# The states of a state-space mixer stored by planes of the step index, its powers moved behind the stacking of u, and a third piece of the gated projection between the halves

## The chip, the cores and the metric

One Trainium2 chip, one of its cores. The time is device microseconds from launch to end; the time before is the median of three executions.

## The reference

A trunk of two layers over 256 tokens of width 1024. The first layer mixes tokens with a diagonal complex state-space model and a gated projection, the second with differential attention; behind each stands a mixture of 32 experts in 4 groups. Only the first mixer is touched:

```
u = rms_norm(x) @ w_in                         # 64 groups of 16 channels
lam_bar = exp(lam * dt)                        # per group, 64 complex states
b_bar = ((lam_bar - 1) / lam) * b
s[t] = lam_bar * s[t-1] + b_bar @ u[t]         # complex
y = real(c @ s) + d_skip * u
val, gate = split(gelu(y) @ w_glu, 2)
x = x + val * sigmoid(gate)
```

## The kernel before

All is fp32 in the mixer. Four engines and SyncE (SP, which only issues transfers) run programs of their own and meet at semaphores; each program's order is written out by hand, and an engine that waits holds up everything behind. `then_inc` raises a semaphore, `wait_ge` waits for a value.

The 256 time steps are taken four at a time (SB = 4), so that the recurrence runs over M = 64 steps, m = 8 h + l: h counts eight segments, l eight steps within one (SEG = 8). Two groups make a pair, 32 pairs, worked on in four octets o of eight (OCT). One pair's two times 64 states fill the 128 partitions; re and im are i = 0, 1. A half is two octets.

- `inputs(c)`, TensorE: u for 128 channels into PSUM. `stack`: copies u out of PSUM into U4, 4 steps x 32 channels on the partitions, 64 copies, 56 of them on ScalarE (ACT) and the last 8 on VectorE (DVE).
- `weights(o)`, VectorE, makes input weights W1 from powers of lam_bar; `turn_w1`, TensorE, turns them; `keep_w1T`, ScalarE, copies them back. GpSimd (POOL) makes the output weights W2 for all octets at the same time, and clears tiles before and after.
- mu: lam_bar^4 to its eighth powers, VectorE: three calls of `powers`, each six products (`cmul`).
- `drive(o)`, TensorE: the inputs of the recurrence into PSUM (v_done, two per octet); `keep_x(o)`, ScalarE, copies them to X.
- `taps(o)`, TensorE: the direct part of y within four steps; `skips(half)`, VectorE, adds d_skip; `own(half)`, ScalarE, copies the result to Fw.
- `local_states(half)`, VectorE: within each segment x[l+1] += mu x[l], seven steps of five operations (`advance`: three products, two sums). `carries(half)`: from segment to segment, six steps of the same form on 32 elements. `carried(o)`: adds to each state what its segment was handed, four products and two sums per octet, and raises `state`.
- `y(o)`, TensorE: U4 times Fw, which needs `f_ready`, then X times W2, which needs `state`. Then `gelu` (ScalarE), `turn_g` (TensorE), `keep_g` (ScalarE).
- `glu(n, ks)`, TensorE: the gated projection for token tile n % 2 and column half n // 2, k in ks of eight. y(0) and y(1) give k 0 to 3, y(2) and y(3) give k 4 to 7. Behind it sigmoid (ScalarE) and product and sum (VectorE, `mixed`).

X lies as [re/im, pair, m]: neighbouring l are adjacent, and the operands of local_states (one l, all h) step by 8 words.

Behind the mixer come norm, router and experts. 2 MB units of expert weights go through nine slots; the first eight units wait for tiles of the mixer that they overwrite, the next for experts that are done.

## Time and profile before

| | us |
|---|---|
| median of 3 (lowest, highest) | 950.24 (949.27, 950.56) |
| profiled execution: time, span | 950.29, 948.5 |
| TensorE busy | 736.2 |
| VectorE busy | 302.0 |
| ScalarE busy | 186.5 |
| GpSimd busy | 75.1 |
| mixer: end of its last projection | 207.7 |

The busy times are sums over the whole span, and the stages have different limits; what counts is which wait ends last in a stage. The chain is the way back from the last instruction, at each step to what released it. The clock is TensorE's granted clock as a share of 2.4 GHz. Durations of pipelined operations overlap, so steps are read from one start to the next.

### The profile page before, as it was taken

Reading aid. Unit: us, or ns where it says so; the run is one execution under the profiler, and the core shown is the slowest. Engines: PE = TensorE matmul, PEld = TensorE weight load, DVE = VectorE, ACT = ScalarE, POOL = GpSimd, SP = SyncE. Lnnn points to the kernel's source line nnn. Section 1 sums busy time; section 2 is a strip of 40 time slices with the busy share of each in tenths; the row PEclk is TensorE's granted clock in tenths of the full one; section 3 lists DMA queues with packets and bytes.
Section 4 is the critical chain, followed back from the end, with each engine's and each line's share of the span. In section 5 each row is a group of like instructions: output and inputs, shape, how many; then the busy total and the mean of one; then the engine's idle time right before and its main releaser. Section 6 shows DMA issues by size and latency. Waiting matters only on the chain.

```text
span 948.5 us, 15405 instructions
## 1 busy us (share of the span) xinstructions
PE 736.2 (78%) x6273; PEld 432.3 (46%) x6273; DVE 302.0 (32%) x702; ACT 186.5 (20%) x398; POOL 75.1 (8%) x64
## 2 busy tenths in 40 slices
PE   2969485994697668676699996666398999996696
PEld 1859354432554334343344444333354555553453
DVE  5792997115421001100421533223711111211112
ACT  3653430123110000000300324113210111110012
POOL 6691000002100000000000000001200000000000
PEclk9986797995699888878899997877599999999899
DMA  9520502934399999999990472016089990499991
GB/s 262 148 96 1 179 1 75 419 130 197 103 425 425 424 424 423 424 424 423 390 338 1 178 266 89 0 41 247 1 352 423 420 402 0 158 422 424 422 418 63
DMA packets 58074, 238.40 MB, mean 251 GB/s; under 512 B 17624, under 2 KB 17824, under 8 KB 33440
## 3 DMA queue, kind: packets, MB, share of 16 engines
q1 hardware_dynamic: 56560, 235.25, 62.2%
q0 software_dynamic: 576, 2.10, 0.6%
q8 instruction: 41, 0.67, 0.3%
q10 hardware_dynamic: 880, 0.23, 0.1%
q14 instruction: 17, 0.14, 0.0%
HBM read 236.53 MB, written 1.05 MB: 250 GB/s over the span
## 4 chain that ended last, share of the span: by engine, by line
PE 49%; DVE 19%; SPq 16%; DMA 10%; ACT 3%; issue 2%; ACTq 0%; DVEq 0%
SPq L369 16%; PE ps L1573 9%; PE ps L1504 9%; DMA work<-in_moe_w_down 6%; PE ps L1539 5%; PE ps L1439 4%; PE ps L1486 4%; PE ps L1546 4%; DMA ring<-in_moe_w_down 3%; PE ps L1638 3%; PE ps L1360 1%; PE ps L1295 1%; PE ps L1468 1%; DVE work L961 1%; DVE work L962 1%
## 5 line engine op out<-in xcount | busy, mean ns | idle before, releaser
L1504 PE MATMUL ps<-ring,work 128*32 128x256 f32 x1824 | 148.5, 421 | 34.9 <-DMA ring<-in_moe_w_up 24.0
L1504 PEld LDWEIGHTS ps<-ring,work 128*32 128x32 f32 x1824 | 79.9, 121 | 79.9 <-issue 54.9
L1154 DVE TENSOR_TENSOR work<-ps,work 128x256 f32<-128x256 f32 x21 | 12.9, 616 | 300.4 <-PE ps L1504 300.4
L1504 PE MATMUL ps<-work 128*32 128x256 f32 x864 | 87.1, 425 | 27.5 <-DMA ring<-in_moe_w_up 10.8
L1546 PE MATMUL ps<-work 128*128 128x512 f32 x168 | 77.7, 605 | 0.0
L1486 PE MATMUL ps<-work,hT 128*128 128x128 bf16 x736 | 71.2, 227 | 6.7 <-DVE work L1104 6.7
L1504 PEld LDWEIGHTS ps<-work 128*32 128x32 f32 x864 | 45.5, 122 | 62.7 <-issue 44.3
L1573 PE MATMUL ps<-ring,hT 128*128 128x512 f32 x160 | 70.4, 593 | 0.0
L1539 PE MATMUL ps<-ring,work 128*32 128x512 f32 x496 | 65.5, 595 | 6.1 <-DMA work<-in_moe_w_down 4.4
L1486 PE MATMUL ps<-work 128*128 128x128 bf16 x368 | 68.3, 227 | 0.0
L1486 PEld LDWEIGHTS ps<-work,hT 128*128 128x128 bf16 x736 | 59.6, 102 | 15.8 <-issue 8.6
L1439 PE MATMUL ps<-ring,xr 128*128 128x512 f32 x128 | 55.3, 593 | 0.5 <-issue 0.5
L1546 PEld LDWEIGHTS ps<-work 128*128 128x128 f32 x168 | 30.2, 189 | 47.7 <-issue 30.1
L706 ACT COPY work<-ps 128x512 f32<-128x512 f32 x21 | 12.3, 585 | 169.6 <-PE ps L1515 169.6
L1573 PEld LDWEIGHTS ps<-ring,hT 128*128 128x128 f32 x160 | 29.7, 190 | 34.1 <-issue 34.0
L1439 PEld LDWEIGHTS ps<-ring,xr 128*128 128x128 f32 x128 | 24.2, 190 | 30.4 <-issue 30.4
L703 ACT ACTIVATE work<-ps 128x256 f32<-128x256 f32 x21 | 8.1, 383 | 150.3 <-PE ps L1504 150.3
L1486 PEld LDWEIGHTS ps<-work 128*128 128x128 bf16 x368 | 37.6, 102 | 0.0
L1161 DVE COPY work<-ps 128x512 f32<-128x512 f32 x21 | 14.5, 692 | 71.6 <-PE ps L1539 71.6
L1295 PE MATMUL ps<-con,xr 128*128 128x128 f32 x64 | 14.6, 404 | 27.7 <-DVE xr L864 16.7
L1539 PEld LDWEIGHTS ps<-ring,work 128*32 128x32 f32 x496 | 16.7, 109 | 40.5 <-issue 39.4
L451 POOL DMA_DIRECT2D gains<-in_final_norm_g x1 | 0.5, 530 | 400.4 <-DVE x L1255 400.4
(288 smaller groups left out, 990.0 us busy)
## 6 DMA issues: line engine op xcount, KB each, us to landing
ring<-in_moe_w_gate SPq DMA_DIRECT2D x24, 2048.0 KB, 25.3
ring<-in_moe_w_down SPq DMA_DIRECT2D x23, 2048.0 KB, 15.4
ring<-in_moe_w_up SPq DMA_DIRECT2D x17, 2048.0 KB, 23.1
work<-in_moe_w_up SPq DMA_DIRECT2D x15, 2048.0 KB, 22.9
work<-in_moe_w_down SPq DMA_DIRECT2D x9, 2048.0 KB, 27.6
work<-in_moe_w_gate SPq DMA_DIRECT2D x8, 2048.0 KB, 25.9
ring<-in_attn_w_qkv SPq DMA_DIRECT2D x5, 2048.0 KB, 21.2
ring<-in_ssm_w_glu SPq DMA_DIRECT2D x4, 2048.0 KB, 8.8
```

The source lines that it names most:

```text
L369: sp.dma_start(places[slot_of(i)].rearrange("p (e n) -> p e n", e=2), src).then_inc(here, 16)
L706: act.copy(turned_both, ps[:, 7, :]).then_inc(back_ready, 1)
L1154: TTo(hid.rearrange("s (k p) -> s p k", k=2), ps[:, 7, 0:256].rearrange("s (p k) -> s p k", k=2), sil.rearrange("s (p k) -> s p k", k=2), ...
L1161: dve.tensor_copy(yy[:, 0:512], ps[:, 6, :]).then_inc(y0_ready, 1)
L1295: ins = pe.transpose(ps[:, (4 if i else 0) + k // 2, 256 * (k % 2) + P * tt:256 * (k % 2) + P * tt + P], xr[:, tt, k, :], ident)
L1439: ins = mm(ps[:, 4 + 2 * (n % 2) + half, :], gT[:, k, tt * P:(tt + 1) * P], win[u][:, k, :], start=(k == 0), stop=(k == KD - 1))
L1486: ins = mm(ps[:, 4 + k // 4, P * (k % 4):P * (k % 4) + P], parts[i][:, tt, k, :], sel[:, tt, :], start=(tt == 0 and i == 0), stop=(tt == T ...
L1504: ins = mm(ps[s, 6 + j // 2, 0:256], xg[:, k, s], pairs[slots[e // 2]][:, e % 2, k, :], start=(k == 0), stop=(k == KD - 1))
L1539: ins = mm(ps[s, 6 + half, :], hidT[:, P * k + 32 * e:P * k + 32 * e + 32], downs[slots[e // 2]][:, e % 2, k, 512 * half:512 * half + 512] ...
L1546: ins = mm(ps[:, 2 * tt + half, :], swT[:, P * tt:P * tt + P], yy[:, 512 * half:512 * half + 512], start=False, stop=True, skip_group_chec ...
L1573: ins = mm(ps[:, c if tt == 0 else c % 2, :], hT[:, k, tt * P:(tt + 1) * P], win[slot][:, k, :], start=(k == 0), stop=(k == KD - 1))
L1638: ins = mm(ps[:, bank, :], oT[:, k, b * P:(b + 1) * P], win[slot][:, k, :], start=(k == 0), stop=(k == KD - 1))
```

## The change

- **Planes.** X becomes [re/im, l, pair, h], so that one l of all h and pairs is contiguous. U4 takes its columns in the order (l, h); `stack` and `keep_g` do the reordering. carried() writes its result to a tile of its own, Xs, as [re/im, pair, (l h)], which y() reads. Xs lies in slots 4 and 5 of the ring, so the first expert units wait for y_done.
- **Order on VectorE.** weights(2), weights(3) and the eight stack copies come ahead of the powers mu. VectorE copies the inputs of octets 0 and 1 to X itself (`inputs_kept`), ScalarE those of octets 2 and 3. skips(0) goes between the fourth and fifth local step, skips(1) ahead of the carries.
- **Order on TensorE.** drive(2) ahead of the last turn, taps(0) and taps(1) ahead of drive(3). Taps now lie in banks 6 and 7.
- **Projection.** glu(2, k 0 to 3) goes ahead of y(2); the tiles are finished in the order 0, 2, 1, 3.
- **Start.** Half of W2 is cleared by VectorE at the very start, the other half by POOL behind the norm; ssm_d gets a semaphore of its own.

```diff
-        X = part(12288, 64 * M).rearrange("p (i r m) -> p i r m", i=2, r=PAIRS)
+        X = part(12288, 64 * M).rearrange("p (i l r h) -> p i l r h", i=2, l=SEG, r=PAIRS)
...
+        Xs = [pre[:, 6144 + 1024 * n:7168 + 1024 * n].rearrange("p (i r m) -> p i r m", i=2, r=OCT) for n in range(PAIRS // OCT)]
...
+        GLU_OUT = (4, 6, 0, 4)
+        GLU_ORDER = (0, 2, 1, 3)
...
-            ups = ps[:, b, :].rearrange("p (c m s) -> p c m s", c=2, s=SB)
-            dst = U4[32 * j:32 * j + 32, :, :].rearrange("p (c a) m -> p c a m", a=4)[:, 2 * b:2 * b + 2, quad, :]
-            return copy(dst, ups[32 * quad:32 * quad + 32, :, :, SB - 1 - j])
+            ups = ps[:, b, :].rearrange("p (c h l s) -> p c l h s", c=2, l=SEG, s=SB)
+            dst = U4[32 * j:32 * j + 32, :, :].rearrange("p (c a) (l h) -> p c a l h", a=4, l=SEG)[:, 2 * b:2 * b + 2, quad, :, :]
+            return copy(dst, ups[32 * quad:32 * quad + 32, :, :, :, SB - 1 - j])
...
+        def inputs_kept(copy, o, b):
+
+            src = ps[:, 2 * (o % 2) + b, :].rearrange("p (r i l h) -> p i l r h", r=4, i=2, l=SEG)
+            pr = slice(OCT * o + 4 * b, OCT * o + 4 * b + 4)
+            for i in range(2):
+                copy(X[:, i, 0, pr, 1:SEG], src[:, i, SEG - 1, :, 0:SEG - 1])
+                ins = copy(X[:, i, 1:SEG, pr, :], src[:, i, 0:SEG - 1, :, :])
+            return ins
...
-            sp.wait_ge(state, 4)
+            sp.wait_ge(y_done, 4)
...
-            sp.wait_ge(glu_done, 2)
+            sp.wait_ge(glu_done, 3)
...
-            clear(part(4096, 8192), 8)
+            pool.wait_ge(normed, 2)
+            clear(part(8192, 4096), 4)
...
+            pool.wait_ge(half_clear, 1)
...
-            dma(drep[0:8, :], a["ssm_d"][0].rearrange("(c p) -> c p", p=P), s_lam)
+            dma(drep[0:8, :], a["ssm_d"][0].rearrange("(c p) -> c p", p=P), s_d)
...
-            act.wait_ge(s_lam, 64)
+            act.wait_ge(s_lam, 48)
...
             keep_w1T(2, 0)
-            keep_x(0)
             keep_w1T(2, 1)
             keep_w1T(3, 0)
-            keep_x(1)
             keep_w1T(3, 1)
             keep_x(2)
...
-                act.copy(gT[:, 2 * o:2 * o + 2, :].rearrange("p c (m s) -> p c s m", s=SB),
-                         ps[:, o, :].rearrange("p (s c m) -> p c s m", s=SB, c=2)).then_inc(g_ready, 1)
+                for c in range(2):
+                    ins = act.copy(gT[:, 2 * o + c, :].rearrange("p (h l s) -> p s l h", h=SEG, s=SB),
+                                   ps[:, o, :].rearrange("p (s c l h) -> p c s l h", s=SB, c=2, l=SEG)[:, c])
+                ins.then_inc(g_ready, 1)
...
+            for k in range(4):
+                ins = dve.memset(part(4096 + 1024 * k, 1024), 0.0)
+            ins.then_inc(half_clear, 1)
...
+            weights(2)
+            weights(3)
+            dve.wait_ge(u_done, 8)
+            for n in range(8):
+                stack(dve.tensor_copy, 3, n).then_inc(u4_ready, 1)
             link(dve.tensor_copy(mu[:, 0:2, 0, :], Pw[:, 0:2, 4, :]))
             powers(mu, 1, 1, 0, 0)
             powers(mu, 2, 2, 1, 0)
             powers(mu, 4, 4, 3, 0)
             link(TS(mu[:, 2, :, :], mu[:, 1, :, :], -1.0, None, ALU.mult))
-            weights(2)
-            weights(3)
-            dve.wait_ge(u_done, 8)
-            for n in range(8):
-                stack(dve.tensor_copy, 3, n).then_inc(u4_ready, 1)
+            for o in range(2):
+                for b in range(2):
+                    dve.wait_ge(v_done, 2 * o + b + 1)
+                    link(inputs_kept(dve.tensor_copy, o, b))
+                    dve.sem_inc(v_kept_x, 1)
...
+            def skips(half):
+
+                dve.wait_ge(k_done, 2 * half + 2)
+                taps = ps[:, 6 + half, :].rearrange("p (q n) -> p q n", q=KD // 2)[:, :, 0:PC]
+                TTo(taps, taps, skip[:, 4 * half:4 * half + 4, :], ALU.add).then_inc(k_ready, 1)
+
...
-                seg = X[:, :, rs, :].rearrange("p i r (h l) -> p i r h l", l=SEG)
                 tmp = [v[:, 0:256].rearrange("p (i r h) -> p i r h", i=2, r=16) for v in (scanP, scanQ)]
-                dve.wait_ge(v_kept_x, 4 * half + 4)
+                if half:
+                    dve.wait_ge(v_kept_late, 4)
                 for l in range(1, SEG):
                     n = SEG if l < SEG - 1 else SEG - 1
-                    dst = seg[:, :, :, :, l + 1] if l < SEG - 1 else seg[:, :, :, 1:SEG, 0]
+                    dst = X[:, :, l + 1, rs, :] if l < SEG - 1 else X[:, :, 0, rs, 1:SEG]
                     by = lambda i: spread(spread(mu[:, i, 0, rs], 1, 2), 3, n)
-                    advance(dst, seg[:, :, :, 0:n, l], tmp[0][:, :, :, 0:n], tmp[1][:, :, :, 0:n], by)
+                    advance(dst, X[:, :, l, rs, 0:n], tmp[0][:, :, :, 0:n], tmp[1][:, :, :, 0:n], by)
+                    if l == 4 and half == 0:
+                        skips(0)
...
-                seg = X[:, :, pr, :].rearrange("p i r (h l) -> p i r h l", l=SEG)
                 flat = hT[:].rearrange("p k t -> p (k t)")
                 n = 2 * OCT * SEG * (SEG - 1)
-                tmp = [flat[:, n * k:n * k + n].rearrange("p (i r h l) -> p i r h l", i=2, r=OCT, h=SEG) for k in range(2)]
-                by = lambda i: spread(mu[:, i, 0:SEG - 1, pr].rearrange("p n r -> p r n"), 2, SEG)
-                start = lambda i: spread(seg[:, i, :, :, 0], 3, SEG - 1)
+                tmp = [flat[:, n * k:n * k + n].rearrange("p (i l r h) -> p i l r h", i=2, l=SEG - 1, r=OCT) for k in range(2)]
+                by = lambda i: spread(mu[:, i, 0:SEG - 1, pr], 3, SEG)
+                start = lambda i: spread(X[:, i, 0, pr, :], 1, SEG - 1)
                 for i in range(2):
                     TTo(tmp[0][:, i], start(i), by(0), ALU.mult)
                     ins = TTo(tmp[1][:, i], start(1 - i), by(1 if i else 2), ALU.mult)
                 link(ins)
-                dst = X[:, :, pr, :].rearrange("p i r (h l) -> p i (r h) l", l=SEG)[:, :, :, 1:SEG]
-                for v in tmp:
-                    link(TTo(dst, dst, v.rearrange("p i r h l -> p i (r h) l"), ALU.add))
+                dst = X[:, :, 1:SEG, pr, :].rearrange("p i l r h -> p i l (r h)")
+                if o == 0:
+                    dve.wait_ge(w2_ready, 4)
+                for i in range(2):
+                    dve.tensor_copy(Xs[o][:, i, :, 0:SEG], X[:, i, 0, pr, :])
+                link(TTo(dst, dst, tmp[0].rearrange("p i l r h -> p i l (r h)"), ALU.add))
+                for i in range(2):
+                    ins = TTo(Xs[o][:, i, :, SEG:64].rearrange("p r (l h) -> p l r h", h=SEG), X[:, i, 1:SEG, pr, :], tmp[1][:, i], ALU.add)
+                link(ins)
                 dve.sem_inc(state, 1)
...
                 local_states(half)
                 if half == 0:
-                    skips(0)
+                    skips(1)
                 carries(half)
-                if half == 0:
-                    skips(1)
                 carried(2 * half)
...
-                done = {(0, 1): 2, (1, 0): 4, (1, 1): 6, (2, 0): 8, (3, 0): 10, (3, 1): 12}
+                done = {(0, 1): 2, (1, 0): 4, (1, 1): 6, (2, 0): 8, (3, 0): 10, (3, 1): 14}
...
+            drive(2)
             turn_w1(3, 1)
-            drive(2)
+            taps(0)
+            taps(1)
             drive(3)
-            for o in range(4):
-                taps(o)
+            taps(2)
+            taps(3)
...
-                        ins = mm(rows(r), X[:, i, OCT * o + r, :], W2[:, i, OCT * o + r, :], start=False, stop=(i == 1),
+                        ins = mm(rows(r), Xs[o][:, i, r, :], W2[:, i, OCT * o + r, :], start=False, stop=(i == 1),
...
+            glu(0, range(4))
             pe.wait_ge(f_ready, 32)
-            glu(0, range(4))
             glu(1, range(4))
+            glu(2, range(4))
             y(2)
             y(3)
             turn_g(2)
             turn_g(3)
             glu(0, range(4, KD))
...
+            glu(2, range(4, KD))
             glu(1, range(4, KD))
             pe.wait_ge(mixed, 1)
-            glu(2, range(KD))
-            pe.wait_ge(mixed, 2)
             glu(3, range(KD))
 
```

VectorE behind weights(1), with what each row waits for (dve_steps is its own chain): before, the powers (ring<-ring; the first and the last shown) come first, then weights(2) and (3), the stack copies, and the first local step.

```order
L945 COPY ring<-work 128x2x32 [waits dve_steps]
L893 TENSOR_TENSOR ring<-ring 128x32 [waits dve_steps]
...
L949 TENSOR_SCALAR ring<-ring 128x256 [waits dve_steps]
L931 TENSOR_TENSOR ring<-ps,ring 128x384 [waits w1_turned,dve_steps]
...
L935 TENSOR_TENSOR ring<-ring,ps 64x8x3x16
L335 COPY gains<-ps 32x2x64 [waits dve_steps,u_done]
L335 COPY gains<-ps 32x2x64 x7
L958 TENSOR_TENSOR hT<-work,ring 128x256 [waits v_kept_x]
```

Now the last product of weights(3), the stack copies, the powers, the input copies, the first local step.

```order
L953 TENSOR_TENSOR ring<-ring,ps 64x8x3x16
L340 COPY gains<-ps 32x2x64 [waits dve_steps,u_done]
L340 COPY gains<-ps 32x2x64 x7
L968 COPY ring<-work 128x2x32
L911 TENSOR_TENSOR ring<-ring 128x32 [waits dve_steps]
...
L972 TENSOR_SCALAR ring<-ring 128x256 [waits dve_steps]
L347 COPY work<-ps 128x4x7 [waits v_done,dve_steps]
L348 COPY work<-ps 128x7x32
L347 COPY work<-ps 128x4x7
...
L348 COPY work<-ps 128x7x32
L981 TENSOR_TENSOR hT<-work,ring 128x256 [waits dve_steps]
```

The powers' 19 rows moved from ahead of two weights() to behind the stack copies, and 16 input copies stand between them and the recurrence.

TensorE from the seventh input projection (L1316) on, before: turns (L1348), drives (L1360), turns, drives, then the first taps (L1377).

```order
L1348 MATMUL ps<-con,ring 128x128 x8
L1316 MATMUL ps<-hT,ring 128x256 x8
L1348 MATMUL ps<-con,ring 128x128 x16
L1360 MATMUL ps<-gains,ring 128x64 x32
L1348 MATMUL ps<-con,ring 128x128 x16
L1360 MATMUL ps<-gains,ring 128x64 x32
L1377 MATMUL ps<-ring,work 32x32
L1377 MATMUL ps<-ring,xr 32x32
L1377 MATMUL ps<-work 32x96
L1377 MATMUL ps<-work,xr 32x96
```

Now (lines are 29 higher):

```order
L1377 MATMUL ps<-con,ring 128x128 x8
L1344 MATMUL ps<-hT,ring 128x256 x8
L1377 MATMUL ps<-con,ring 128x128 x16
L1389 MATMUL ps<-gains,ring 128x64 x32
L1377 MATMUL ps<-con,ring 128x128 x8
L1389 MATMUL ps<-gains,ring 128x64 x16
L1377 MATMUL ps<-con,ring 128x128 x8
L1406 MATMUL ps<-ring,work 32x32
L1406 MATMUL ps<-ring,xr 32x32
L1406 MATMUL ps<-work 32x96
```

drive(2) comes ahead of the last turn, and taps follow it at once; the fourth drive stands behind 64 rows of taps.

TensorE from y(1)'s state part (L1418) on, before: gelu's turns (L1426), two pieces of the projection (L1439), y(2), y(3), turns, the rest.

```order
L1418 MATMUL ps<-work 64x128 x16
L1426 MATMUL ps<-con,work 128x128 x8
L1439 MATMUL ps<-ring,xr 128x512 x16
L1412 MATMUL ps<-work,gains 64x128 x8
L1418 MATMUL ps<-work 64x128 x16
L1412 MATMUL ps<-work,gains 64x128 x8
L1418 MATMUL ps<-work 64x128 x16
L1426 MATMUL ps<-con,work 128x128 x8
L1439 MATMUL ps<-ring,xr 128x512 x48
```

Now:

```order
L1449 MATMUL ps<-work,ring 64x128 x16
L1457 MATMUL ps<-con,work 128x128 x8
L1470 MATMUL ps<-ring,xr 128x512 x24
L1443 MATMUL ps<-work,gains 64x128 x8
L1449 MATMUL ps<-work,ring 64x128 x16
L1443 MATMUL ps<-work,gains 64x128 x8
L1449 MATMUL ps<-work,ring 64x128 x16
L1457 MATMUL ps<-con,work 128x128 x8
L1470 MATMUL ps<-ring,xr 128x512 x40
```

Eight products moved from behind y(2) and y(3) to ahead of them: 24 + 40, where there were 16 + 48.

## Rows read from the trace of the kernel before

**Rows 1.** The page: the span, and the chain's shares by engine.

```profile
span 948.5 us, 15405 instructions
...
PE 49%; DVE 19%; SPq 16%; DMA 10%; ACT 3%; issue 2%; ACTq 0%; DVEq 0%
```

**Rows 2.** The chain in order of time: start us, us, what.

```profile
163.66 0.60 PE ps L1426 x4
...
166.48 41.22 PE ps L1439 x96
...
252.04 7.11 PE ps L1504 x128
...
283.91 8.10 SPq L369
```

**Rows 3.** Timeline, VectorE, 85 to 125: start us, us, line, operation, idle before.

```profile
89.91 0.62 DVE L958 TENSOR_TENSOR hT<-work,ring 128x256 f32<-128x256 f32 x1 [17.82 <-ACT work L607]
...
107.81 0.20 DVE L958 TENSOR_TENSOR hT<-work,ring 128x32 f32<-128x32 f32 x1
...
113.24 0.30 DVE L1006 TENSOR_TENSOR ps<-ps,work 128x128 f32<-128x128 f32 x1
```

**Rows 4.** Timeline, TensorE, 125 to 145: y and the first half of the projection.

```profile
125.20 3.33 PE L1418 MATMUL ps<-work 128*64 128x128 f32 x32 [1.63 <-DVEq L1000]
...
130.36 13.97 PE L1439 MATMUL ps<-ring,xr 128*128 128x512 f32 x32 [0.50 <-issue]
...
144.26 1.58 PE L1412 MATMUL ps<-work,gains 128*64 128x128 f32 x16
```

**Rows 5.** Timeline, 0 to 25: the start of the program on POOL and VectorE.

```profile
6.95 7.51 POOL L463 MEMSET work<- 128x1024 f32 x8
...
8.90 0.93 DVE L842 TENSOR_SCALAR work<-work 32x128 f32<-32x128 f32 x1
...
14.46 4.08 DVE L864 SCALAR_TENSOR_TENSOR xr<-x,small,gains 128x1024 f32<-128x1024 f32 x2
...
20.02 0.21 DVE L870 TENSOR_SCALAR work<-work 32x128 f32<-32x128 f32 x1
```

**Rows 6.** Timeline, TensorE, and line 1377: projection, turns, drives, taps.

```profile
55.18 1.04 PE L1348 MATMUL ps<-con,ring 128*128 128x128 f32 x8
...
56.05 3.62 PE L1316 MATMUL ps<-hT,ring 128*128 128x256 f32 x16
...
88.50 7.26 PE L1360 MATMUL ps<-gains,ring 128*128 128x64 f32 x64
...
L1377 PE MATMUL ps<-work,xr x64: 246/246/246, 96.0 to 104.7; 128*32 128x96 f32 x64
```

**Rows 7.** Timeline, VectorE, 45 to 72: powers, weights(2), stacking.

```profile
45.61 0.74 DVE L945 COPY ring<-work 128x64 f32<-128x64 f32 x1
...
53.89 1.25 DVE L893 TENSOR_TENSOR ring<-ring 128x128 f32<-128x128 f32 x1
...
60.43 0.56 DVE L931 TENSOR_TENSOR ring<-ps,ring 128x384 f32<-128x384 f32 x1
...
69.60 2.48 DVE L335 COPY gains<-ps 32x128 f32<-32x128 f32 x8 [0.15 <-DVE ring L935]
```

**Rows 8.** Timeline, POOL, 71 to 76: clearing behind its products.

```profile
71.67 3.62 POOL L463 MEMSET work<- 128x1024 f32 x4 [0.15 <-POOL work L489]
```

**Rows 9.** Timeline, VectorE, 148 to 154: carrying into one octet.

```profile
148.36 0.92 DVE L994 TENSOR_TENSOR hT<-work,ring 128x448 f32<-128x448 f32 x1
...
151.79 2.22 DVE L999 TENSOR_TENSOR work<-work,hT 128x896 f32<-128x896 f32 x2
```

**Rows 10.** Windows: us from:to, length, busy of each engine, TensorE's clock, DMA, GB/s.

```profile
79.00:86.00 7.00, 7.00 (x35) 7.00 (x35) 0.00 (x0) 3.02 (x6) 0.00 (x0) 0.50 0.00 0
...
105.00:110.00 5.00, 0.00 (x0) 0.00 (x0) 0.30 (x1) 1.92 (x7) 0.81 0.75 274
```

**Rows 11.** Line 335, stacking: count, ns min/median/max, first to last start, forms.

```profile
L335 ACT COPY gains<-ps x56: 253/257/259, 39.7 to 61.7; 32x128 f32<-32x128 f32 x56
```

More of the change, by code:

```diff
@@ L673, in _ @@
             keep_g(3)
[L675 to L679 removed]
+            for turn_no, n in enumerate(GLU_ORDER):
+                act.wait_ge(glu_done, turn_no + 1)
+                if turn_no >= 1:
+                    act.wait_ge(mixed, turn_no)
+                act.activation(sig[:, 0, :], ps[:, GLU_OUT[n] + 1, :], ACT.Sigmoid).then_inc(sig_ready, 1)
             def moe(l):
@@ L711, in moe @@
                 return passes_through(act, l)
-            norm(1, mixed, 3, 4)
+            norm(1, mixed, 2, 4)
             total = moe(0)
@@ L1322, in turn_params @@
                 pe.wait_ge(lam_ready, 1)
+                pe.wait_ge(s_d, 16)
                 for n in range(4):
@@ L1432, in glu @@
                 for k in ks:
-                    if n < 2 and k % 2 == 0:
+                    if k % 2 == 0:
                         pe.wait_ge(g_ready, k // 2 + 1)
```

44 lines of the change are left out of this document (18 added, 26 removed).

## The prediction

> **What bounds the kernel now.** I read the page first: the span is 948.5 us and its chain is half TensorE, a fifth VectorE, the rest weight streaming [rows 1]. Then the chain in order of time: up to the router it goes through the state-space mixer, which ends with the gated projection at 166.48 + 41.22 = 207.7 us; the stream of expert weights enters only at 283.9, after the first passes have freed their slots [rows 2]. Nothing in the mixer waits for the stream, and the stream's start hangs on the mixer's end. So what the mixer saves is saved at the end, one for one, and I price the mixer alone.
>
> Inside it, VectorE's timeline is the thing to see. The recurrence starts at 89.91, after 17.82 us of idleness; its seven local steps last until 107.6, 2.55 us each; the carries take 5.4 (107.81 to 113.24) [rows 3]. Carrying into one octet takes (151.79 - 148.36) + 2.22 + 0.2 = 5.85 [rows 9], twice in a half. That makes 17.7 + 5.4 + 11.7 = 35 us a half, in one unbroken run of short operations, each waiting for the one before. TensorE waits for the second half too: the U part of y(2) is done at 145.84 [rows 4] and the chain has y(3) end only at 163.66 [rows 2].
>
> **The start of the program.** POOL clears 8 pieces from 6.95 to 14.46 [rows 5]. Meanwhile a scalar operation on VectorE over 32x128 takes 0.93 (0.21 where POOL is idle), and five such stand ahead of the norm's products, which start at 14.46 [rows 5]. At most 5 x 0.72 = 3.6 us are to be had; some hides behind ScalarE's squares. The change puts four of the pieces on VectorE at the very start, ahead of its first work, and four on POOL behind the norm. I take 2.2 us for everything up to the stacking, ends 0 and 2.9. ssm_d on a semaphore of its own is in that figure.
>
> The Trainium skill (SBUF — State Buffer, "SBUF: two separate sides") says that VectorE's two-port operations and GpSimd share a port pair as a lock held for a whole instruction. The trace agrees (0.93 against 0.21 us). [...]
>
> **Up to the recurrence.** The last input projection now ends at 56.05 + 3.62 - 2.2 = 57.5 [rows 6]. weights(2) and weights(3) come ahead of the powers. weights(3) waits for the fourth turn, which ended at 56.2, so 54.0 [rows 6]; one takes (69.60 - 60.43)/2 = 4.6 [rows 7], so 58.6. The eight stack copies take 2.5 [rows 7]: 61.1, where before they ended at 72.1. The powers follow. While POOL multiplies, copy and first two powers took 45.61 to 53.89, 8.3 us [rows 7]; POOL's products end at 71.67 - 2.2 = 69.5 [rows 8], so this stretch stays dear and ends at 69.4. The third power is six products of 128; a free one has 0.30 [rows 3], overlapped 0.2, so 1.4. One scalar operation beside POOL's clearing takes 1.0 (as the 0.93). The powers end at 71.8. Moving them saves no work. It lets drive(0) start at 61 and not 72.
>
> Then VectorE copies the inputs of octets 0 and 1 itself: 16 copies, 4 each of four times. No row has 28 or 224 elements. With 0.15 + 1.04 ns per element (0.30 for 128 [rows 3], 0.56 for 384 [rows 7], 1.1 for 896 [rows 9]), a set is 2 x 0.18 + 2 x 0.38, less what overlaps, 0.88; four are 3.5 (2.5 to 6 if the PSUM reads are stepped at half rate). TensorE's drives are done long before: 64 passes take 7.26 at the full clock [rows 6], so 61.1 to 68.4. The recurrence starts at **75.3**, 14.6 earlier.
>
> **The recurrence.** In the old layout neighbours in h lie 32 bytes apart: 256 elements take 0.62, 448 take 0.92, about 1.8 ns each, where contiguous ones have 1.04 [rows 3, 9]. By planes the three products and sums of 256 take 0.42 and the two of 128 lose 0.09 each: 0.8 less per step, 1.75. Seven steps are 12.1 (was 17.7). The carries keep their stride and step: 5.4. Carrying into an octet: four products 0.92 to 0.62, minus 1.2; added are two copies of 64 (0.25), and the second sum is now two instructions (0.05): 5.85 to 4.95.
>
> The Trainium skill (Vector Engine (DVE) Microarchitecture Reference, "Measured stream behaviour on trn2") gives about 1.04 ns per column for adjacent words and up to 2.5 where a stream steps by a few words. By that a step would save 1.3 and not 0.8; only the first half's seven steps lie on the path, so the sum would be 921.4. The rows have 1.8, and they decide.
>
> **New waits.** skips(0) stands after the fourth step, at 75.3 + 7.0 = 82.3, and waits for taps 0 and 1. drive(2) can start when octet 0 is copied, 73.6; +3.6, a turn 1.0, two taps of 2.3 (four of them keep TensorE from 95.7 to 104.9, and of their last kind of matmul the first starts at 96.0, the last at 104.7 [rows 6]): 82.9. With the sum itself 83.3; three more steps, 88.4. skips(1) now stands ahead of the carries and waits for all taps: drive(3) 86.5, two taps 91.1. That is a new stall of 2.7 us on VectorE, with the carries, states and y(0) queued behind it. Carries 91.5 to 96.9; states 1 and 2 at 101.9 and **106.8** (before 125.1, just ahead of the matmuls at 125.20 [rows 4]). ScalarE copies octets 2 and 3 and then both blocks of taps, free at about 102, in time.
>
> **The gated projection.** From state 2 to its first matmul are 5.25 us (125.1 to 130.36 [rows 4]). TensorE's clock adds: after the taps it is idle and falls, as in 105 to 110 (0.81, on its way to 0.5) [rows 10]. y(0)'s X part then runs at 1.2 GHz, 5.3 and not 3.33, and y(1)'s U part falls behind state 2: +2.3 (0 to 3). Start 114.4; with gelu and turning as before. Three pieces of k 0 to 3 are 24 products at 13.97/16 = 0.87 [rows 4]: 20.9, till 135.3. State 4 is there at 106.8 + 12.1 + 5.4 + 9.9 = 134.2, so in the second half VectorE no longer bounds. y(2) and y(3), each 1.58 + 3.33 [rows 4]: 145.1. Turning took 163.66 to 166.48 [rows 2]: 147.9. Left are 40 products at 41.22/48 = 0.86 [rows 2], 34.4: **182.3** against 207.7. The third piece alone shortens the tail by 6.9. The new order of tiles gains nothing behind it, since ScalarE takes the four sigmoids first in either order. The expert DMAs: the first pair goes at 145, the last at 182, and 9 units of 2 MB need some 45 us; they are first used some 45 us after the projection (at 252.04 before [rows 2]), and so stay free.
>
> **Sum.** 25.4 us less. The profiled execution took 950.29 (span 948.5 [rows 1], and 1.8 around it); the median of three is 950.24, the same to 0.01%. So **924.9**. By parts: 14.6 until the recurrence starts and 5.6 + 1.8 in its first half, less some 3.7 for the waits for taps, are 18.3 at state 2; less 2.3 for the clock, 16.0 where the projection starts. The other 9.4 come out of the gap between its halves: y(2), y(3) and turning took 144.3 to 163.7 with the waits for states 3 and 4, 19.4 us, and take 9.8 once the third piece fills the wait. The products themselves are as many as before.
>
> **Rivals.**
> - *Clock lost before drive(2)* (0.2). TensorE idles from 69.5 to 73.6. An idle stretch had lowered the clock before the drives of 79 to 86, and these ran at 0.50, 1.2 GHz, to their end without raising it [rows 10]. In the idle 105 to 110 the mean is still 0.81: the clock fell in the course of it, and whether 4.1 us suffice is open. If they do, drive(2), a turn and two taps cost twice their time, 3.6 + 1.0 + 4.6 = 9.2 more, ahead of skips(0): 934. If it stays low until the last taps, another 8.2: 942.
> - *Better than the sum* (0.17). Clock still up at y(0) (2.3), the full 2.9 at the start (0.7), no wait for the taps because the input copies overlap better (up to 2): 919 to 922.
> - *Stepped reads cost* (0.08). The stack now reads PSUM 128 bytes apart (before 16; 0.257 us for 128 elements [rows 11], full rate). At double, ScalarE gets 48 x 0.11 = 5 us more, most of it hidden behind the powers that wait for POOL; with input copies at 6 and not 3.5 it is 928 to 931.
> - *Slower than before* (0.03). The same copies, but dear: 48 of them stand on ScalarE ahead of the last, in series with the turns that TensorE waits for. From 0.9 us a copy, three and a half times the row, 48 x 0.64 eats slack and gain; at 1.2 it is about 965. The Trainium skill (PSUM — Partial Sum Buffer, "Specifications") warns that non-contiguous patterns in PSUM slow matmuls; of copies it says nothing.
> - *No change* (0.02). The saved time comes back as waiting for expert weights: 950. Against it the 45 us above: the stream has as long a lead as before.
>
> The forecast itself (921 to 929) has 0.5. Range 915 to 935: it leaves out the two last, half of the clock rival and a little below. A measurement of this kernel tells 0.2%, 1.9 us, from none: faster 0.95, same 0.02, slower 0.03.
>
> **What the new profile would show.** The norm's products near 12.3; drive(0) near 61 at clock 1.0; powers slow until about 69.5; recurrence from 75, products of 256 at 0.42; two waits of VectorE for taps, 0.6 and 2.7; state 2 near 107; 48 passes of projection in one block without TensorE waiting for states 3 and 4; projection done at 182, and all behind it shifted as a block. Wrong would make it: drive(2) at 0.5; the powers or input copies past 76; products of 256 still at 0.6; stack copies over 0.4.

## The result, and the profile after

The changed kernel takes **920.29 us**, median of four executions (914.15 to 924.4), against 949.75 of the kernel before measured beside it (949.13 to 950.56): ratio 0.968 [0.963, 0.974]. The profiled execution is the slowest of the four, 924.4 us, span 922.6. With eleven more executions from the experiments the fifteen of the changed kernel have a median of 922.0 and lie between 913.9 and 924.9, a spread of 11 us where thirty-five of the kernel before had 4.2. This spread is the second thing that had to be explained.

The page and the chain of the kernel after, which answer to [rows 1, 2]:

```profile
span 922.6 us, 15451 instructions
...
PE 55%; SPq 16%; DVE 11%; DMA 11%; ACT 5%; issue 2%; ACTq 0%; DVEq 0%
```

```profile
147.34 34.35 PE ps L1470 x80
181.71 0.60 ACT work L694
...
226.11 7.11 PE ps L1535 x128
...
257.98 8.05 SPq L383
```

VectorE's share of the chain fell from 19% to 11%. The last product of the projection ends at 181.7, before at 207.7: 26.0 us earlier. The passes behind the router start at 226.1 (before 252.0), the stream's next piece of the chain at 258.0 (before 283.9): all 25.9, and the span is 25.9 shorter. What the mixer saved was saved at the end, one for one.

VectorE in the changed kernel (start us, us, line, operation, idle before), against [rows 3, 9]:

```profile
76.66 0.43 DVE L981 TENSOR_TENSOR hT<-work,ring 128x256 f32<-128x256 f32 x1
...
78.44 0.43 DVE L981 TENSOR_TENSOR hT<-work,ring 128x256 f32<-128x256 f32 x1
...
87.27 0.30 DVE L991 TENSOR_TENSOR ps<-ps,work 128x128 f32<-128x128 f32 x1 [3.52 <-PE ps L1406]
...
93.85 0.30 DVE L991 TENSOR_TENSOR ps<-ps,work 128x128 f32<-128x128 f32 x1 [1.21 <-PE ps L1406]
...
99.56 0.62 DVE L1024 TENSOR_TENSOR hT<-work,ring 128x448 f32<-128x448 f32 x1
...
104.48 0.63 DVE L1024 TENSOR_TENSOR hT<-work,ring 128x448 f32<-128x448 f32 x1 [0.16 <-DVE ring L1034]
...
109.39 0.42 DVE L981 TENSOR_TENSOR hT<-work,ring 128x256 f32<-128x256 f32 x1 [0.15 <-DVE ring L1034]
```

The recurrence starts at 76.66 in place of 89.91. A product of 256 elements takes 0.43 and not 0.62 us, a local step 78.44 - 76.66 = 1.78 and not 2.55, carrying into an octet 104.48 - 99.56 = 4.92 and not 5.85. Twice VectorE waits for taps (L1406 is their line): 3.5 and 1.2 us. State 2 is there at 109.2.

TensorE in the same stretch, against [rows 4]:

```profile
62.06 7.33 PE L1389 MATMUL ps<-gains,ring 128*128 128x64 f32 x64 [1.57 <-DVE gains L340]
69.22 1.04 PE L1377 MATMUL ps<-con,ring 128*128 128x128 f32 x8
...
74.67 7.06 PE L1389 MATMUL ps<-gains,ring 128*128 128x64 f32 x32 [4.40 <-DVEq L977]
...
98.61 2.88 PE L1443 MATMUL ps<-work,gains 128*64 128x128 f32 x16 [4.86 <-ACT work L634]
104.43 5.48 PE L1449 MATMUL ps<-work,ring 128*64 128x128 f32 x29 [2.94 <-DVEq L1036]
...
115.71 20.87 PE L1470 MATMUL ps<-ring,xr 128*128 128x512 f32 x48 [0.40 <-ACT xr L676]
```

and its granted clock there (stretch, length, TensorE's busy time, clock, DMA share, GB/s):

```profile
70.00:72.00 2.00, 0.27 (x3) 1.00 0.00 0
72.00:74.00 2.00, 0.00 (x0) 0.51 0.00 0
74.00:84.00 10.00, 9.33 (x56) 0.50 0.01 2
84.00:87.00 3.00, 3.00 (x120) 0.72 0.02 5
...
96.00:108.00 12.00, 6.45 (x37) 0.50 0.66 247
```

64 passes of the drives take 7.33 us at 62, the next 32 take 7.06 at 74.7: the same work a pass, at half the clock. This is the rival of the prediction that had 0.2, here in the profiled execution. The projection starts at 115.7 (before 130.36), its three pieces run in one block, y(2) follows without a wait.

### The profile page after: what moved, and what is told of

The parts are those of the page before. It is cut to its first block, busy times and chain, and to the rows that moved or that the text cites. A ratio compares the mean times of both kernels' runs of the same rounds, so it can differ in the third digit from the quotient of the medians.

```text
span 922.6 us, 15451 instructions
## 1 busy us (share of the span) xinstructions
PE 728.2 (79%) x6273; PEld 425.5 (46%) x6273; DVE 287.8 (31%) x734; ACT 185.2 (20%) x410; POOL 71.3 (8%) x60
## 4 chain that ended last, share of the span: by engine, by line
PE 55%; SPq 16%; DVE 11%; DMA 11%; ACT 5%; issue 2%; ACTq 0%; DVEq 0%
SPq L383 15%; PE ps L1535 10%; PE ps L1604 9%; PE ps L1470 6%; PE ps L1570 5%; PE ps L1517 5%; PE ps L1577 4%; DMA ring<-in_moe_w_down 4%; DMA ring<-in_moe_w_up 3%; PE ps L1669 3%; DMA work<-in_moe_w_down 3%; PE ps L1449 2%; PE ps L1499 1%; PE ps L1323 1%; PE ps L1389 1%
## 5 line engine op out<-in xcount | busy, mean ns | idle before, releaser
L1604 PE MATMUL ps<-ring,hT 128*128 128x512 f32 x160 | 70.4, 593 | 0.0
L1344 PE MATMUL ps<-hT,ring 128*128 128x256 f32 x128 | 30.9, 400 | 1.3 <-ACT hT L583 1.3
```

What stands on the lines that cost most here:

```text
L1344: ins = mm(ps[:, c // 2, 256 * (c % 2):256 * (c % 2) + 256], win[c // 4][:, k, P * (c % 4):P * (c % 4) + P], hT[:, k, :], start=(k == 0), ...
L1604: ins = mm(ps[:, c if tt == 0 else c % 2, :], hT[:, k, tt * P:(tt + 1) * P], win[slot][:, k, :], start=(k == 0), stop=(k == KD - 1))
```

## Why the executions spread: two repetitions

Both are the changed kernel unedited; each brings five or six times and one profile.

> The changed kernel again, nothing edited. Its four executions so far lay between 914.2 and 924.4 us, those of the kernel before between 949.1 and 950.6. The profiled one is the slowest of them, and in it TensorE's granted clock was 0.50 while the drives of octet 2 (7.06 us for 32 products) and the X part of y(0) (5.48 us) ran. Theory A (the clock): the executions differ in whether the clock is still 1.00 at these two places; then a profile with a time near 918 shows one of the two at 1.00, one near 914 both, and with drives at 1.00 their 32 products take 3.6 us. Theory B (the rest of the program): the spread lies behind the projection; then the last sigmoid ends at 181.7 +- 0.5 us in a faster execution too, and the stretch from it to the end, 740.9 us in the profiled one, is the shorter. Median under both 917 to 923.

> The changed kernel once more, as the companion of the three other runs and for one more profile. Ten executions so far: 913.9 to 924.9 us. The profiles so far show what differs between executions of one program: the first product takes 5.8 or 3.7 us, log_dt lands at 7.2 to 8.2 us, and the clock falls at once after the gap of 4.4 us (72 us, twice), early in it (69.4), or already in the drives of 64 columns ahead of it (63 to 65 us, twice), and in one of these last two it was up again before the drives of octet 2, which then did not keep VectorE waiting. Theory (these draws make the spread): a profiled time of 913 to 916 shows the second set of drives at 1.00 and both waits for the taps under 1 us; one of 918 to 921 shows the first product at 3.7 us or the waits gone, not both; one of 923 to 925 neither. Rival: the stretch behind the last sigmoid, which was 738.0 to 742.8 us in the profiles so far, makes the difference.

Measured: 923.75 us (913.93 to 924.86, profiled 924.86) and 921.42 (919.78 to 924.41, profiled 921.42). The three profiles of the changed kernel and those of the four fastest variants, read at the same places (us from the span's start; the first column of numbers is the profiled execution's time):

| profiled run | us | first product | drives start | clock falls | waits for taps | projection starts | last sigmoid | from there to the end of the span |
|---|---|---|---|---|---|---|---|---|
| changed | 924.4 | 5.75 | 62.1 | 72 | 4.7 | 115.7 | 181.7 | 740.9 |
| same | 924.9 | 5.79 | 62.2 | 72 | 4.7 | 115.9 | 181.9 | 741.2 |
| same_again | 921.4 | 3.7 | 59.1 | 72 | 4.3 | 112.4 | 178.4 | 741.2 |
| warm_start | 916.3 | 5.34 | 61.1 | 64 | 0 | 110.5 | 176.5 | 738.0 |
| late_skips | 918.1 | 3.69 | 59.2 | 69 | 0 | 107.5 | 173.5 | 742.8 |
| late_skips_own | 916.1 | 5.40 | 60.6 | 63 | 0 | 110.0 | 176.0 | 738.3 |
| short_gap_fill | 917.6 | 3.69 | 58.7 | 72 | 4.3 | 112.1 | 178.1 | 737.7 |

Three things differ from profile to profile ("draws" below). First, the start: the first input product takes 3.7 us or 5.3 to 5.8, and log_dt lands at 6.6 to 8.1 us; same and same_again differ by 3.1 us at the drives and by 3.5 at the last sigmoid. The product's draw looks like the clock's. The trace has no record of the granted clock before 17 us (warm_start's fill aside), and the record, at full clock, begins at 17.4 to 19.0 us in every profile of this study with a product of 3.7 us, at 22.4 to 26.2 in those with a slow one (in warm_start the clock comes back at 22.8); in same_again it begins at 17.6, where the last two transposes take 387 and 283 ns after 421 for those before them. Second, the clock at drive(2), with VectorE's waits behind it: 0 or 4.3 to 4.7 us. Third, the rest of the program, 737.7 to 742.8 us between the last sigmoid and the end. In it TensorE's clock was at the lower level for 154 to 158 us in the three shortest and for 164 to 172 in the four others, so the clock goes with this draw too, though no run shows that it makes it.

The best of all three from the profiled 924.4 would be 924.4 - 3.1 - 4.7 - 3.2 = 913.4, and the fastest executions have 913.9 and 914.2. This is a sum over different profiles, not an execution seen: no profile of the changed kernel caught one below 921. In its three profiles the clock fell ahead of drive(2) or 0.5 us into it and the rest took 740.9 to 741.2 us; the good values of the second and third draw come from variants alone. So neither theory of the first expectation was put to its test, and it had not named the start, the only draw that the three profiles show. The second expectation gave 918 to 921 us to a profile with one good draw; same_again has one and 921.4.

## Experiments on the clock before drive(2)

**warm_gap, warm_both.** Filling products in TensorE's idle stretches:

```diff
             turn_w1(3, 0)
+            pe.wait_ge(w1T_ready, 12)
+            warm(6, range(9))
             drive(2)
```

(`warm` multiplies the identity by 512 columns of U4, once for each number of the range, into a bank that nothing uses then), and for warm_both 13 more behind taps(3) and 7 between y(0)'s two parts.

> The changed kernel with nine more products of 512 columns on TensorE (identity by the stacked u, into a bank that nothing uses then) between the last transposes of octet 3's first half and the drives of octet 2, where TensorE idled 4.4 us for the input copies. At 0.43 us each (the projection's products at full clock) they end just ahead of these copies. Theory A (the clock falls because TensorE idles there): the drives of octet 2 run at 1.00 and take 3.6 us in place of 7.06, VectorE's waits for the taps, 3.5 and 1.2 us, shrink to under 1.5 in sum, state 1 comes 3 to 4 us earlier, and the time is 915 to 918 with a spread between executions below 4 us. Rival A2 (the clock falls because the drives of 64 columns ahead of the gap count as little work): the clock still falls to 0.50 some way into the drives of octet 2, and the time stays at 918 to 923. Rival B (nothing of the drives is on the path): the drives are faster, the time is unchanged.

> As the run with nine filling products, and 13 more behind the last taps and 7 more between the two parts of y(0), where TensorE idled 4.9 us for the local Toeplitz blocks and 2.9 us for state 1. Theory A: y(0)'s X part then runs at 1.00 and takes 2.9 us in place of 5.48, 2.3 to 2.6 us less than the run with nine alone: 912.5 to 915.5 us, and no execution above 918. Rival (the fill comes too long and holds y(0) back): state 1 is there while filling products still run, and the time is 1 to 3 us above theory A's. Rival B (y(0)'s clock is not on the path since state 2 ends it): time as with nine alone.

Measured: 922.53 (920.22 to 928.93) and 930.54 (925.23 to 935.64), with the changed kernel beside them at 923.75 (same): no gain, and a loss of 7 us. The edit was mis-sized: I had read 0.43 us, the mean of one record, as one product, but a product of 512 columns leaves two records. Nine take 7.8 us at full clock, not the 3.9 that I had reckoned for a gap of 4.4. The profile of warm_gap shows more (TensorE's timeline):

```profile
60.60 11.65 PE L1389 MATMUL ps<-gains,ring 128*128 128x64 f32 x64 [1.57 <-DVE gains L340]
...
73.75 9.36 PE L1413 MATMUL ps<-gains,con 128*128 128x512 f32 x18
82.95 3.68 PE L1389 MATMUL ps<-gains,ring 128*128 128x64 f32 x32
```

Here the clock was 0.50 from 63 on, in the middle of the drives of 64 columns, with only 1.57 us of idleness ahead of them. It came back during the fill, drive(2) ran at full speed (3.68), but 8.3 us later than in the changed kernel (82.95 against 74.67); VectorE waited 8.2 us for the taps. In warm_both's profile the clock stayed at 1.00 from 60 to 118, y(0)'s X part took 2.9, and yet the projection started only at 117.3, since the fills ran until 100.8 and 108.6. Here the high clock, bought with work on the same engine's path, cost more than it returned.

**short_gap_fill.** The same with three products.

> The changed kernel with three filling products of 512 columns in the gap of 4.4 us ahead of the drives of octet 2. A product of 512 columns is 0.87 us at full clock (7.73 us for nine in warm_both) and 1.73 at half, so that the nine of warm_gap and warm_both were twice too long for the gap and held the drives back by 3.3 us and more; three take 2.6 us at full clock. Theory A (the clock falls because of the gap): it stays at 1.00 through the drives of octet 2, VectorE's waits for the taps fall from 4.7 us to under 1, the time is 915 to 918 with a spread below 5 us. Theory A2 (the drives of 64 columns count as little work, and the fall is a draw with or without the gap): the times spread as the changed kernel's, 914 to 925, and where the clock falls in the drives ahead of the gap, the fill takes 5.2 us and costs 0.8.

Measured: 921.65 (917.62 to 921.92); the changed kernel beside it 921.42. Timeline and clock of TensorE:

```profile
66.77 2.74 PE L1413 MATMUL ps<-gains,con 128*128 128x512 f32 x6
71.31 6.39 PE L1389 MATMUL ps<-gains,ring 128*128 128x64 f32 x32 [1.80 <-DVEq L977]
```

```profile
71.00:72.00 1.00, 0.69 (x6) 1.00 0.00 0
72.00:73.00 1.00, 1.00 (x7) 0.52 0.07 16
```

The fill ran at full speed, only 1.8 us of idleness were left, and the clock fell all the same, with drive(2) already running. So a gap of 4.4 us is not needed for the fall. The drives (64 columns to a weight load) are not the whole cause either: the clock fell 2.5 to 2.7 us into the first of them in warm_start, warm_gap and late_skips_own, in changed and same 1.8 us into the idleness that follows them and a turn, but in old_start (below) at 63.2, just as the first drive began, behind turns and 1.6 us of idleness. When the fall comes (63 to 72 us) differs from execution to execution, and what sets it stays open.

**warm_start.** Three filling products ahead of the first transposes:

> The changed kernel with three products of 512 columns (identity by x, into a bank unused then) ahead of the first transposes, as soon as x and the constants have landed. The transposes of the normed x take 244 ns each in all profiles so far (3.9 us for 16) and the first product of the inputs 5.75 us in two executions of the changed kernel and 3.69 us in three of the kernels derived from it; transposes later on take 110 ns at a granted clock of 1.00 and 214 ns at 0.50. Theory A (TensorE starts slow, and whether it comes up before or after the first product is a draw that makes part of the spread of 10 us): with the fill 2 us go from the first product in every execution, perhaps 1.9 more from the transposes, the upper end falls to 921 or below and the median to 917 to 920. Rival (the fill ends after the normed x is there): transposes start later than 15.0 us, 0 to 2 us lost. Rival (the spread is elsewhere): median 920 to 923, range 914 to 925.

```profile
7.25 5.49 PE L1333 MATMUL ps<-x,con 128*128 128x512 f32 x6 [7.25 <-DMA con<-in_con]
14.28 1.09 PE L1323 MATMUL ps<-con,xr 128*128 128x128 f32 x8 [1.54 <-DVE xr L882]
16.28 1.97 PE L1323 MATMUL ps<-con,xr 128*128 128x128 f32 x8 [0.91 <-DVE xr L882]
19.50 5.34 PE L1347 MATMUL ps<-hT,ring 128*128 128x256 f32 x16 [1.25 <-ACT hT L583]
```

Measured: 919.01 (916.28 to 925.2). The fill runs at 1.83 us a product, half speed; the first eight transposes are fast (1.09), the next eight slow again (1.97), and the first product slow too. The granted clock was 1.00 from 12.6 to 16.0 us and 0.50 from there to 22.8, so the fill brought TensorE to full speed for a moment and did not keep it there. The 916.28 of the profiled execution has another cause, which the timeline shows further on:

```profile
61.07 11.39 PE L1392 MATMUL ps<-gains,ring 128*128 128x64 f32 x64 [1.57 <-DVE gains L340]
...
73.95 3.73 PE L1392 MATMUL ps<-gains,ring 128*128 128x64 f32 x32
```

The clock fell at 64, early in the drives. They took 11.39 us in place of 7.33, but VectorE was still at its powers, so nobody waited; the gap before drive(2) closed, the clock was back at 74 (0.99 in 74 to 76), and drive(2) ran in 3.73. The taps were done in time. The early fall is the good draw (late_skips_own has it too, at 63.4): it costs where there is slack and is over where there is none. The expectation is not confirmed; whether the median moved can't be told against 11 us of spread.

## Experiments on the waits for the taps

**late_skips** moves the two sums on VectorE behind more of its own work:

```diff
-                    if l == 4 and half == 0:
+                    if l == 6 and half == 0:
                         skips(0)
...
                 local_states(half)
+                carries(half)
                 if half == 0:
                     skips(1)
-                carries(half)
```

> The changed kernel with VectorE's skips(0) behind step 6 of the local recurrence in place of step 4, and skips(1) behind the carries in place of ahead of them. In the profiled execution VectorE waited 3.5 us and 1.2 us for the taps there. Theory A (these waits are on the path): both waits go, state 1 and state 2 come 4 to 4.7 us earlier in an execution with the drives at the low clock, 916 to 920 us in such a one; one with the clock at 1.00 at the drives gains about 1 us or nothing. Rival (the taps are only waited for because TensorE is late, and ScalarE's own blocks, which begin behind skips(0), then become what y(0) waits for): f_ready ends y(0)'s wait in place of state 1, and the time is unchanged or up to 2 us worse.

Measured: **916.26** (914.56 to 918.14), ratio 0.965 [0.963, 0.967]. Both waits are gone (no idleness in the rows), although drive(2) was slow in this execution too (7.06):

```profile
84.51 0.30 DVE L991 TENSOR_TENSOR ps<-ps,work 128x128 f32<-128x128 f32 x1
...
91.91 0.30 DVE L991 TENSOR_TENSOR ps<-ps,work 128x128 f32<-128x128 f32 x1
```

From the recurrence's first step to the projection's first product are 33.7 us, in the changed kernel 39.0: 5.3 less, of which 4.7 are the waits. The waits were on the path. The spread of the times shrinks from 11 us to 3.6 (4.9 with the ten executions of this kernel and the next), which fits a draw that has lost its hold; but the five of same_again alone lay within 4.6 us, so this reading is argued, not shown. The rival had a point: y(0)'s U part now waits for ScalarE's own blocks until 95.8.

**late_skips_own** puts these blocks (own(0)) ahead of ScalarE's keep_x(3).

> The kernel of late_skips (skips(0) behind step 6, skips(1) behind the carries), and on ScalarE the first half's own blocks ahead of the last two copies of inputs, which octets 0 and 1 do not need. In the profile of late_skips these blocks ran from 89.5 to 95.7 us and y(0) waited for them, not for state 1. Theory (they are the bound there): they run from 84.9 to 91.1, y(0)'s first part starts then, state 1 ends y(0)'s wait and state 2 y(1)'s, the projection starts 1.1 us earlier relative to the start of the recurrence (33.7 us from its first step to the projection's first product in late_skips, 32.6 here), and the time is 914 to 916. Rival (TensorE idles between the two parts instead, the clock falls there as before, and y(0)'s X part ends as late): the same 33.7 and 916.

Measured: 916.09 (914.46 to 919.37), no difference to late_skips; the ten executions of the two have a median of 916.2. The blocks came earlier, TensorE then idled before the X part and did it at half clock, as the rival had it. Between the landmarks it even lost: from the recurrence's first step to the projection's first product are 34.8 us (110.0 - 75.2), where late_skips had 33.7 and the theory 32.6.

```profile
98.35 5.66 PE L1449 MATMUL ps<-work,ring 128*64 128x128 f32 x29 [2.12 <-DVEq L1036]
```

## Experiments on the parts of the change

No changed kernel ran beside the first three of these four, so their steps are read in the profiles, between landmarks of the same profile.

**powers_first** puts the powers back ahead of weights(2).

> The changed kernel with the powers of the multipliers back ahead of weights(2), nothing else. In the profile of the changed kernel they take 10.5 us beside GpSimd's products. Theory A (the order is worth what the prediction said, in part): weights(3) ends near 70 in place of 59.3, the drives start near 72.5 in place of 62.1, but the recurrence, which needs the powers and the input copies, starts near 81 in place of 76.7; the projection starts 4.4 us later, and the time is 4 to 5 us above the changed kernel's: 925 to 928. Rival (the order is worth nothing, since the recurrence waits for the sum of both on VectorE): within 1 us. Rival (TensorE is the bound there): 10 us above.

Measured: 931.91 (930.79 to 932.55), 4 us more than expected.

```profile
68.26 13.89 PE L1389 MATMUL ps<-gains,ring 128*128 128x64 f32 x64 [0.70 <-DVE gains L340]
```

```profile
DVE work L347 <- PE ps L1389: 11.4, 4, 3.8
```

TensorE waits 7.6 us for weights(2) and (3), its clock falls (0.83 in 58 to 60, then 0.50), and the drives need 13.9 us. Now VectorE waits for the drives between its input copies (11.4 us). The recurrence starts at 83.2, and that with the good draw at the start (first product 3.7). So the order is worth about 9.7 us at the projection's start (123.3 + 2.1 for the draw, against 115.7). The drives' longer time, 13.9 - 7.3 = 6.6 us, is most of it, since VectorE waited for the drives to their end: the clock, lost in TensorE's waits, cost more than the order of VectorE's work itself.

**old_layout** stores the states as before and undoes all copies and reads that go with it.

> The changed kernel with the states stored by pair, step and segment in one run of 64 as in the kernel before, and with it the stacking, the copies of the inputs, the recurrence, the reading by TensorE and the copy behind the turning as they were; order of work, third piece and start as changed. Theory A (steps at 2.55 us for 1.78): a half's local states 5.4 us longer and each octet's carried states 0.9, but VectorE's waits for the taps, 3.5 and 1.2 us in the profiled execution, vanish, so that the projection starts 2 to 3 us later; the second half's states end some 9.8 us later, near 146.7, and y(3) waits for them: the last sigmoid 5 us later, and the time 925 to 928. Rival (stores and reads that step by 8 words cost nothing where the engine waits anyway): within 1 us of the changed kernel. Rival (all of 2 x 7.3 us shows): 933 or more.

Measured: 928.32 (926.11 to 929.66). A product of 256 takes 0.62 again:

```profile
L975 DVE TENSOR_TENSOR hT<-work,ring x8: 196/616/625, 75.5 to 94.5; 128x256 f32<-128x256 f32 x6, 128x224 f32<-128x224 f32 x1, 128x32 f32<-128x32 f32 x1
```

From the recurrence to the projection 41.2 us (39.0 changed), from there to the last sigmoid 70.4 (66.0): together 6.6 dearer, expected 5. In the first half most of the 7.3 us is swallowed by the waits for the taps (0.9 left of 4.7); in the second y(2) and y(3) wait 1.5 and 1.6 us for their states, as the expectation had it for y(3).

**two_pieces** leaves the third piece of the projection out of the gap.

> The changed kernel without the third piece of the gated projection between the halves: its first eight products of 512 columns stand behind y(2) and y(3) again, as in the kernel before. Worked out from the profile of the changed kernel: the two pieces left end at 129.6 us in place of 136.5, y(2) has to wait for state 3 (132.0) and y(3) for state 4 (136.9), y(3) ends at 139.7 and not 144.5, and 48 products follow where 40 did (41.7 us against 34.4). Theory A (the piece fills a wait): the last sigmoid ends 2.4 us later, 184.1, and the time is 2 to 3 us above the changed kernel's median of 920 to 923: 923 to 926. Rival (the piece only moves, since the half's states end the gap either way): no difference. Rival (it loses): 1 us or more below the changed kernel.

Measured: 922.28 (920.57 to 923.17). TensorE's timeline:

```profile
113.53 14.00 PE L1470 MATMUL ps<-ring,xr 128*128 128x512 f32 x32 [0.41 <-ACT xr L676]
...
129.76 3.00 PE L1449 MATMUL ps<-work,ring 128*64 128x128 f32 x29 [0.72 <-DVEq L1036]
...
134.68 3.33 PE L1449 MATMUL ps<-work,ring 128*64 128x128 f32 x32 [0.60 <-DVEq L1036]
```

From the projection's start to the last sigmoid 68.5 us against 66.0: 2.5 dearer, expected 2.4. The median does not show it; this profile has the 3.7 us draw at the start, and 2.5 us is less than a draw.

**old_start** undoes the shared clearing and ssm_d's own semaphore.

> The changed kernel with the start as before: GpSimd alone clears the eight pieces that the changed kernel shares with VectorE, without its wait for the normed x, and ssm_d is waited for with the other parameters. Theory A (1.7 us as the two profiles read): the norm's first operation starts at 14.4 to 14.6 us in place of 12.7, the first product at 21.7 in place of 20.1, and everything behind it 1.7 us later; the time is 1.7 us above the changed kernel's in the same draw of the clock. Rival (the 2.2 us of the prediction): 14.9 and 22.3. Rival (nothing, since the landing of the parameters ends the wait either way): 12.7 to 13.

Measured: 922.59 (921.67 to 926.55), beside it same_again with 921.42: 1.2 us, within what the draws do. The landmarks are clear (VectorE, then TensorE):

```profile
14.46 4.07 DVE L877 SCALAR_TENSOR_TENSOR xr<-x,small,gains 128x1024 f32<-128x1024 f32 x2
```

```profile
21.80 5.37 PE L1339 MATMUL ps<-hT,ring 128*128 128x256 f32 x15 [1.25 <-ACT hT L581]
```

14.46 and 21.80 against 12.74 and 20.1 in the changed kernel: 1.7 us, as the first theory had it. The other variants have 11.4 to 13.0 and 18.8 to 20.2, so the start is worth 1.5 us against the latest of them.

## Point by point: right in the sum, with errors that cancel

The prediction was 924.9 us, range 915 to 935; measured 920.3, with all repetitions 922.0, and the profiled execution, against whose predecessor the sum was made, 924.4. Two executions of fifteen lie under the range. That the time would fall was never in doubt. That the sum came out within 0.5 us of the profiled time is in part luck: state 2 came 2.4 us late (109.2 for 106.8), and two later terms gave back 1.1 and 1.8.

- **The start** (2.2): 1.7. The norm in the changed kernel:

```profile
12.74 4.07 DVE L882 SCALAR_TENSOR_TENSOR xr<-x,small,gains 128x1024 f32<-128x1024 f32 x2
```

  The scalar operations take 0.21 now, and VectorE's work from its first product to the norm takes 4.5 us where it took 6.7: the 2.2 of the forecast. But log_dt lands at 8.0 here, that first product starts at 8.2 and not 7.7, and this took 0.5 back. A gain by ssm_d's semaphore is not to be seen. Beside VectorE's four clears POOL's first seven ended at 7.0, as before, so clears of the two engines did not hold each other up. This agrees with the Trainium skill (SBUF — State Buffer, "SBUF: two separate sides"), by which a VectorE instruction with at most one SBUF input, outside the two-port modes, does not contend with GpSimd.
- **Up to the recurrence** (75.3): 76.66. Stacking ended at 61.9 (61.1); the powers took 10.6 (10.7) and ended at 72.5 (71.8); from there to the recurrence were 4.1 (3.5). The order was right; the stacking came 0.8 late and the copies took 0.6 more.
- **The recurrence**: step 1.78 (1.75), carrying 4.92 (4.95), carries 5.5 (5.4). By the rate of the Trainium skill for stepped words (Vector Engine (DVE) Microarchitecture Reference, "Measured stream behaviour on trn2") a step would have saved 1.3, as the prediction has it; its own 1.04 and 2.5 ns over a step's 1024 elements give an estimate of 1.5. The step saved 0.77, as the rows had it.
- **New waits** (0.6 + 2.7 = 3.3 with the clock up): this step of the prediction failed, twice over. drive(2) ran at 0.50 and took 7.06, not 3.6. And "two taps of 2.3" was mis-sized: the 9.2 us from which it came held 3.44 us of idleness, which the kernel before has in the middle of its taps (below). Two taps take 2.9 us at full clock. With the clock up and this price nothing is waited for, as warm_start shows; with the clock down the waits are 4.7. So the rival came true and costs 4.7 us, 1.4 more than the waits of the forecast, and not its 9.2: it used the same wrong taps, doubled them, and left out that the clock comes back during the taps (0.72 in 84 to 87).
- **y(0) at half clock** (+2.3): seen, 5.48 for the X part, but it cost half of that. From state 2 to the projection's first product were 115.7 - 109.2 = 6.5 us, 1.2 above the 5.25 of before, where 7.6 were forecast: 1.1 given back.
- **Projection start** (114.4): 115.7, 14.6 earlier than before where 16.0 were forecast.
- **The gap between the halves** (9.8 for y(2) and y(3)): 144.5 - 136.5 = 8.0, for the X products of one and the U products of the other stand side by side in the timeline, where the forecast added them up. Before it was 19.4. So 11.4 came from here and not 9.6: 1.8 given back.
- **Stepped PSUM reads** (0.08): they cost nothing, see below. **Expert weights** (0.02): the block behind is shifted as a whole.

## What to carry to other kernels

Before you price a stretch by last start minus first start of a group, look for idleness inside it: here a third of the taps' 9.2 us was. When an engine waits for a sum that is only needed later (the taps' sums), place it behind more of the waiting engine's own work: that gave 4.7 us on the path, which no filling of the clock's gaps did. And when executions of one kernel start to spread, read several profiles at the same landmarks before comparing medians: a step of 2 us is visible between landmarks and not in the medians.

## What the runs showed of the hardware

The idleness inside the taps of the kernel before, with no releaser in the profile; the changed kernel and its variants don't have it:

```profile
103.30 0.22 PE L1377 MATMUL ps<-ring,work 128*32 128x32 f32 x1 [3.44 <-issue]
```

Reading PSUM 128 bytes apart costs a copy nothing: 256 ns for 128 elements as before [rows 11].

```profile
L340 ACT COPY gains<-ps x56: 252/256/260, 38.3 to 60.3; 32x128 f32<-32x128 f32 x56
```

Drives of 64 columns kept TensorE busy without a pause, and still its granted clock fell from 1.00 to 0.50 in them or behind them, at 63 to 72 us, in the profiles of the changed kernel and its variants, three apart: in warm_both it stayed up, in powers_first it was down at 59.3, before them, and in old_start it fell at 63.2, as they began. Five falls came 1.8 to 1.9 us into the idleness behind the turns that follow the first drives (changed, same, late_skips, two_pieces, old_layout), two 0.5 and 0.7 us into drive(2) (same_again, short_gap_fill).

The granted clock's column reads 1.00 at the program's start, while transposes there take 244 ns each, more than twice the 110 ns of later ones at 1.00. That 1.00 is no measurement: the trace has no record of the clock there. In warm_start, where there is one, the same transposes are fast at 1.00 and slow at 0.50.
